# First norm and index tiles of a two-layer trunk, taken in halves of the features

## What is computed

```python
cond = silu(c)
mod = cond @ mod_w[i] + mod_b[i]
sh1, sc1, g1, sh2, sc2, g2 = jnp.split(mod, 6, axis=-1)
h = modulate(rms_norm(x, norm_mix_g[i]), sh1, sc1)   # norm * (1 + sc1) + sh1
proj = h @ w_in                                      # q, k, v, qi, ki, wi
logits = einsum(qi, ki) / 8                          # 8 index heads
score = sum over heads of wi * relu(logits)          # then the 64 best keys per query
```

## Time and profile before

| | |
|---|---|
| profiled execution | 809.15 us, span 807.1 us |
| PE / PEld busy | 744.8 us (92%) / 669.7 us (83%) |
| DVE / ACT / POOL busy | 595.7 (74%) / 389.5 (48%) / 208.2 us (26%) |
| DMA | 157.51 MB, mean 195 GB/s |
| chain that ended last | PE 64%, DVE 19%, issue 8%, ACT 6% |

### The profile page before, as it was taken

How to read it: one execution, slowest core, us unless ns; L and a number is a source line. 1 busy time by engine, 2 the same in 40 slices (tenths; PEclk the granted TensorE clock), 3 DMA queues, 4 the chain that set the end, 5 groups by cost and what they waited for, 6 DMA issues and landing times.

```text
span 807.1 us, 17682 instructions
## 1 busy us (share of the span) xinstructions
PE 744.8 (92%) x6676; PEld 669.7 (83%) x6676; DVE 595.7 (74%) x935; ACT 389.5 (48%) x651; POOL 208.2 (26%) x121
## 2 busy tenths in 40 slices
PE   4589999999899999999999888998999999999996
PEld 0176999667788989898989778997979999999994
DVE  7854555895778888888898886677557776676675
ACT  2254544555464444454444543334456555555554
POOL 5900000121315445544544234552000000000000
PEclk9789999999989999999999989999989999999998
DMA  8869655496726777777765311111644556555531
GB/s 313 345 224 369 215 182 182 184 411 262 266 79 249 251 258 258 260 260 256 256 247 175 134 53 54 54 54 62 201 131 131 184 182 198 168 180 192 171 102 53
DMA packets 45979, 157.51 MB, mean 195 GB/s; under 512 B 6257, under 2 KB 7793, under 8 KB 45937
## 3 DMA queue, kind: packets, MB, share of 16 engines
q1 hardware_dynamic: 43632, 148.55, 52.6%
q10 hardware_dynamic: 1728, 6.29, 2.0%
q0 software_dynamic: 576, 2.10, 0.7%
HBM read 155.87 MB, written 1.05 MB: 194 GB/s over the span
## 4 chain that ended last, share of the span: by engine, by line
PE 64%; DVE 19%; issue 8%; ACT 6%; DMA 2%; POOL 1%; DVEq 0%; ACTq 0%; POOLq 0%
PE up L326 11%; PE up L328 11%; PE up L327 11%; PE acc L326 7%; DVE wlo L978 7%; PE acc L327 7%; PE acc L328 7%; ACT whi L719 3%; PE gv L362 2%; DVE ffn L1232 2%; DMA ffn<-in_mw 1%; DVE hl L1007 1%; DVE diag L999 1%; PE up L667 1%; PE acc L642 1%
## 5 line engine op out<-in xcount | busy, mean ns | idle before, releaser
L978 DVE TENSOR_TENSOR wlo<-raw,whi 128x1024 fp32r<-128x1024 f32 x194 | 304.5, 1586 | 102.0 <-ACT whi L719 100.8
L326 PE MATMUL up<-hh,whi 128*128 128x256 f32 x944 | 272.0, 288 | 4.3 <-DVE hl L1007 3.0
L327 PE MATMUL up<-hl,whi 128*128 128x256 f32 x944 | 269.3, 285 | 0.0
L328 PE MATMUL up<-hh,wlo 128*128 128x256 f32 x944 | 269.2, 285 | 0.0
L719 ACT ACTIVATE whi<-raw 128x1024 fp32r<-128x1024 f32 x194 | 200.9, 1051 | 35.3 <-PE acc L328 24.4
L326 PEld LDWEIGHTS up<-hh,whi 128*128 128x128 f32 x944 | 183.5, 194 | 16.1 <-issue 11.1
L327 PEld LDWEIGHTS up<-hl,whi 128*128 128x128 f32 x944 | 183.7, 195 | 0.0
L328 PEld LDWEIGHTS up<-hh,wlo 128*128 128x128 f32 x944 | 183.4, 194 | 0.0
L326 PE MATMUL acc<-ah,whi 128*128 128x256 f32 x352 | 100.4, 285 | 6.8 <-DVE wlo L978 6.6
L327 PE MATMUL acc<-al,whi 128*128 128x256 f32 x352 | 99.6, 283 | 0.0
L328 PE MATMUL acc<-ah,wlo 128*128 128x256 f32 x352 | 99.5, 283 | 0.0
(11 more groups left out here) (200 smaller groups left out, 915.5 us busy)
## 6 DMA issues: line engine op xcount, KB each, us to landing
raw<-in_w SPq DMA_DIRECT2D x194, 512.0 KB, 3.5
mraw<-in_mw SPq DMA_DIRECT2D x60, 512.0 KB, 6.3
arena<-in_mw SPq DMA_DIRECT2D x12, 512.0 KB, 11.6
tmp<-in_mw SPq DMA_DIRECT2D x6, 512.0 KB, 7.9
ffn<-in_mw SPq DMA_DIRECT2D x6, 512.0 KB, 8.6
tmp<-in_mw ACTq DMA_DIRECT2D x4, 512.0 KB, 7.5
ffn<-in_mw ACTq DMA_DIRECT2D x4, 512.0 KB, 9.6
mraw<-in_mw ACTq DMA_DIRECT2D x4, 512.0 KB, 14.3
```

The source lines that it names most:

```text
L326: pe.matmul(out, w_h, xh, start=first, stop=False, skip_group_check=skip)
L327: pe.matmul(out, w_h, xl, start=False, stop=False, skip_group_check=skip)
L328: return pe.matmul(out, w_l, xh, start=False, stop=last, skip_group_check=skip)
L978: dve.tensor_tensor(wlo[:, n % SPL, :], raw[:, n % RAW, :], whi[:, n % SPL, :].bitcast(F32), ALU.subtract).then_inc(lo_ready, 1)
```

## The change

The first norm and the six index tiles are done for features 0 to 511 and then for 512 to 1,023. The chunks are reordered on the host, so that chunk 0 is the scale and chunk 1 the shift of the first half, and 2 and 3 those of the second. SP loads x first, then chunk 0, three small tensors, chunk 1, three more, the first halves of the six weight tiles, chunks 2 and 3, the second halves. The condition and the parameters are issued from ACT's queue. TensorE takes the norm ahead of gemv 0 and has a PSUM bank for each index tile (`idx_bank`), so that their first halves can stay there while gemv 2 and 3 run. GpSimd's six table steps now wait until all six index tiles are evicted, and ACT takes the sine in four pieces behind tiles 25 to 28. VectorE waits for the tables ahead of the attention masks, which lie on the same memory.

```diff
@@ -180,6 +180,9 @@
+        raw_half = raw[:].rearrange("p s (h c) -> p s h c", h=2)
+        whi_half = whi[:].rearrange("p s (h c) -> p (s h) c", h=2)
+        wlo_half = wlo[:].rearrange("p s (h c) -> p (s h) c", h=2)
@@ -206,6 +209,9 @@
+        first_hi, first_lo, first_used = sem("first_hi"), sem("first_lo"), sem("first_used")
+        ones_in = sem("ones_in")
+        w_first = [sem(f"w_first{j}") for j in range(RAW)]
@@ -242,8 +248,10 @@
-        N_PRM, N_EARLY, N_SMALL = 2, 6, 4
+        N_PRM, N_ONES, N_EARLY, N_SMALL = 2, 3, 3, 4
...
+        idx_bank = [acc[:, 0, 0:T], acc[:, 1, 0:T], acc[:, 2, 0:T], acc[:, 3, 0:T], up[:, 0, 0:T], up[:, 1, 0:T]]
@@ -263,19 +271,30 @@
-            sp_.dma_start(craw[:], t["cond"]).then_inc(cond_in, 16)
-            for dst, name in ((prm[:, 0:PRM_IN, :], "prm"), (jrow[:], "jrow")):
-                sp_.dma_start(dst, t[name]).then_inc(prm_in, 16)
-            load_m(0)
-            for dst, name in ((modb[:], "modb"), (ones[:], "ones"), (ident[:], "ident"), (gains[:], "gains"),
-                              (epsc[:], "epsc"), (picks[:], "picks")):
-                sp_.dma_start(dst, t[name]).then_inc(early_in, 16)
+            def load_half(n, h):
+                sp_.dma_start(raw_half[:, n, h, :], t["w"][n, :, 512 * h:512 * h + 512]).then_inc(
+                    (w_first, w_loaded)[h][n], 16)
+            def load_early(c):
+                for s in range((c - 1) * MS, c * MS):
+                    sp_.dma_start(early[:, s, :], t["mw"][MS + s, :, :]).then_inc(m_early[s], 16)
...
-            for s in range(3 * MS):
-                sp_.dma_start(early[:, s, :], t["mw"][MS + s, :, :]).then_inc(m_early[s], 16)
+            load_m(0)
+            for dst, name in ((ones[:], "ones"), (ident[:], "ident"), (epsc[:], "epsc")):
+                sp_.dma_start(dst, t[name]).then_inc(ones_in, 16)
+            load_early(1)
+            for dst, name in ((modb[:], "modb"), (gains[:], "gains"), (picks[:], "picks")):
+                sp_.dma_start(dst, t[name]).then_inc(early_in, 16)
...
-                load_w(n, free=False)
+                load_half(n, 0)
+            load_early(2)
+            load_early(3)
+            for n in range(RAW):
+                load_half(n, 1)
@@ -400,14 +419,16 @@
-                pe.wait_ge(gm_ready, pairs)
+                if pairs:
+                    pe.wait_ge(gm_ready, pairs)
...
-                pe.wait_ge(mod_col, pairs)
+                if pairs:
+                    pe.wait_ge(mod_col, pairs)
@@ -423,26 +444,36 @@
+            def half(n, h):
+                pe.wait_ge((first_lo, lo_ready)[h], n + 1)
+                for kk in range(4):
+                    k = 4 * h + kk
+                    pe.wait_ge(act_lo, k + 1)
+                    w_h, w_l = whi_half[:, n, kk * P:(kk + 1) * P], wlo_half[:, n, kk * P:(kk + 1) * P]
+                    pe.matmul(idx_bank[n], w_h, hh[:, k, :], start=(k == 0), stop=False, skip_group_check=True)
+                    pe.matmul(idx_bank[n], w_h, hl[:, k, :], start=False, stop=False, skip_group_check=True)
+                    mm = pe.matmul(idx_bank[n], w_l, hh[:, k, :], start=False, stop=(k == KT - 1), skip_group_check=True)
+                mm.then_inc((first_used, slot_used)[h], 1)
...
+            pe.wait_ge(ones_in, 16 * N_ONES)
+            pe.wait_ge(early_in, 16 * N_EARLY)
+            norm(0, 0, None)
...
+            spread_root(0, misc[:, T:2 * T])
...
-            pe.wait_ge(early_in, 16 * N_EARLY)
...
-            norm(0, 1, None)
+            for n in range(RAW):
+                half(n, 0)
+            pe.wait_ge(gm_ready, 1)
...
-            spread_root(0, up[:, 0, 0:T])
...
+            pe.wait_ge(hp_ready, 4)
...
-                if n >= 2:
-                    pe.wait_ge(qkv_ready, n - 1)
-                if n == 0:
-                    project_two((up[:, 0, 0:T], up[:, 1, 0:T]), 0, 0)
-                elif n > 1:
-                    project(up[:, n % 2, 0:T], n)
+                half(n, 1)
@@ -739,7 +770,8 @@
-                act.wait_ge(cols_done, 1 if norm == 0 else C_FFN // 2 if norm == 1 else CH)
+                if norm:
+                    act.wait_ge(cols_done, C_FFN // 2 if norm == 1 else CH)
@@ -754,31 +786,61 @@
+            act.dma_start(craw[:], t["cond"]).then_inc(cond_in, 16)
+            for dst, name in ((prm[:, 0:PRM_IN, :], "prm"), (jrow[:], "jrow")):
+                act.dma_start(dst, t[name]).then_inc(prm_in, 16)
...
+            for k in range(KT):
+                square(0, k)
...
+            act.wait_ge(ones_in, 16 * N_ONES)
+            root(0)
+            def first_half(n, h):
+                act.wait_ge((w_first, w_loaded)[h][n], 16)
+                if h:
+                    act.wait_ge(first_used, n + 1)
+                act.activation(whi_half[:, n, :], raw_half[:, n, h, :], ACT.Copy).then_inc((first_hi, hi_ready)[h], 1)
+            def first_in(k):
+                act.wait_ge(hp_ready, k + 1)
+                sh = 4 + k if k < 4 else 8 + k
+                act.activation(hh[:, k, :], tmp[:, k, :], ACT.Identity, bias=modc[:, sh:sh + 1]).then_inc(act_hi, 1)
+            act.wait_ge(csum, 1)
...
-            for k in range(KT):
-                square(0, k)
-            act.wait_ge(early_in, 16 * N_EARLY)
-            root(0)
+            first_half(0, 0)
+            first_half(1, 0)
+            act.wait_ge(mod_col, 1)
+            for k in range(4):
+                first_in(k)
+            for n in range(2, RAW):
+                first_half(n, 0)
...
-            for n in range(SPL):
-                split_hi(n, ring=False)
+            first_half(0, 1)
+            first_half(1, 1)
...
-            norm_hi(0, 0, 8)
+            for k in range(4, KT):
+                first_in(k)
+            for n in range(2, RAW):
+                first_half(n, 1)
...
-                act.activation(qkv[:, n, :], up[:, n % 2, 0:T], ACT.Copy).then_inc(qkv_ready, 1)
-                split_hi(n + SPL)
+                act.activation(qkv[:, n, :], idx_bank[n], ACT.Copy).then_inc(qkv_ready, 1)
+                if n % 2:
+                    act.wait_ge(w_loaded[n // 2], 16 * 2)
+                    act.activation(whi[:, n // 2, :], raw[:, n // 2, :], ACT.Copy).then_inc(hi_ready, 1)
@@ -793,13 +855,21 @@
-            act.wait_ge(tab_arg, TAB_STEPS)
-            act.activation(tab, tab, ACT.Sin, scale=TWO_PI * (1 - 2 ** -23)).then_inc(tab_ready, 1)
-            with act.Fori(1, N_IN // RAW) as i:
+            def tile_out(n, i=0):
+                act.wait_ge(slot_used, n + RAW * i + 1)
+                act.activation(qkv_f[:, ds((n + RAW * i) * T, T)], up[:, n % 2, 0:T], ACT.Copy).then_inc(qkv_ready, 1)
+                split_hi(n + SPL, i)
+            with act.Fori(1, N_IN // RAW - 1) as i:
...
-                    act.wait_ge(slot_used, n + RAW * i + 1)
-                    act.activation(qkv_f[:, ds((n + RAW * i) * T, T)], up[:, n % 2, 0:T], ACT.Copy).then_inc(qkv_ready, 1)
-                    split_hi(n + SPL, i)
+                    tile_out(n, i)
+            for n in range(N_IN - RAW, N_IN):
+                tile_out(n)
+                part = n - N_IN + RAW - 1
+                if 0 <= part < 4:
+                    act.wait_ge(tab_arg, TAB_STEPS)
+                    piece = tab[:, part * 1024:(part + 1) * 1024]
+                    act.activation(piece, piece, ACT.Sin, scale=TWO_PI * (1 - 2 ** -23)).then_inc(tab_ready, 1)
@@ -1009,7 +1079,7 @@
-                dve.wait_ge(amul_ready, norm + 1)
+                dve.wait_ge(amul_ready, norm + 2)
@@ -1077,25 +1147,47 @@
+            def first_half(n, h):
+                dve.wait_ge((first_hi, hi_ready)[h], n + 1)
+                dve.tensor_tensor(wlo_half[:, n, :], raw_half[:, n, h, :], whi_half[:, n, :].bitcast(F32),
+                                  ALU.subtract).then_inc((first_lo, lo_ready)[h], 1)
+            def first_scale(h):
+                dve.wait_ge(mod_col, h + 1)
+                dve.scalar_tensor_tensor(amul[:, 0, 4 * h:4 * h + 4], modc[:, 8 * h:8 * h + 4], 1.0,
+                                         gains[:, 0, 4 * h:4 * h + 4], ALU.add, ALU.mult).then_inc(amul_ready, 1)
+                dve.wait_ge(amul_ready, h + 1)
+                for k in range(4 * h, 4 * h + 4):
+                    scaled(0, k)
+            def first_low(k):
+                sh = 4 + k if k < 4 else 8 + k
+                dve.wait_ge(act_hi, k + 1)
+                dve.scalar_tensor_tensor(hl[:, k, :], tmp[:, k, :], modc[:, sh:sh + 1],
+                                         hh[:, k, :].bitcast(F32), ALU.add, ALU.subtract).then_inc(act_lo, 1)
...
-            col_out(0)
-            scale_columns(0, 0)
+            dve.wait_ge(ones_in, 16 * N_ONES)
...
-            dve.wait_ge(amul_ready, 1)
...
-            for k in range(KT):
-                scaled(0, k, up[:, 0, 0:T])
-            col_out(1)
-            split_lo(0)
-            split_lo(1)
-            for k in range(KT):
-                low_in(k, 0, 8)
```

(30 more changed lines are left out.)

## The result

The changed kernel takes 831.88 us (median of 4 runs, 830.26 to 833.12) against 811.02 for the kernel before (4 runs, 810.74 to 813.1); the ratio is 1.0257 (95% interval 1.0238 to 1.0275). The first norm and the first index tiles do begin earlier, and the whole gets 2.6% slower.

What follows compares the result with a forecast made beforehand. TensorE, fully busy from 86.5 to 144 us, carries any earlier delay to the end, and GpSimd and VectorE exclude each other. Front -1.6, index stage +21.5, clock +2.1: +22.0 on 809.15 gives 831; own range 822 to 837, reaching down to 818.

Steps and rivals of the forecast that it cites:

- The front's start: TensorE's square sums start once the three small early_in loads have landed behind x and chunks 0 and 1: 19.3 us.
- slow clock twice: Index tiles: the lower clock level at both sets of half tiles, each six costing 10.8 us; 2.3 us lost.
- sixth eviction: ACT's copy of the last of six index tiles out of PSUM, put at 66.8 us; before, 68.43.
- The gain of the front: Up to the sixth eviction: tiles start 12 us sooner but end only 1.6 us sooner.
- The stall: Index stage: VectorE alternates with GpSimd's table steps; split of tile 9 39.4 us after the sixth eviction, costing 21.5.
- The clock: Start of tile 9: TensorE's clock falls while it stands waiting, losing 2.1 us (bounds 0 and 2.4).
- Sum: Whole kernel: -1.6 front, +21.5 index stage, +2.1 clock, giving +22.0 us on the profiled 809.15.
- The sine: ACT's Sin leaves the index stage; its four pieces behind tiles 25 to 28 cost zero.
- Held to the end: Index stage: every table step keeps VectorE out for its whole length; four us more, 835; chance 0.12.
- GpSimd yields: Index stage: a VectorE chain that has the port keeps it to its end; 815 us; chance 0.08.
- Faster: Index stage: head accumulations not held, split of tile 9 within 19.5 us; 807 or 802.5 us; chance 0.06.
- the alternation of one VectorE operation per gap: Index stage: VectorE and GpSimd take turns, one VectorE operation between table steps; split of tile 9 at 39.4 us.

Runs made afterwards that it cites:

- half steps: The changed kernel with the six GpSimd table steps cut into 12 of 128x1024, in the same place: 811.80 us, ratio 1.0015.
- quarter steps: The changed kernel with the six GpSimd table steps cut into 24 of 128x512, in the same place: 811.22 us, ratio 0.9998.

## Why the prediction was right

The forecast was 831, the median is 831.88, and the steps it was made of can be held against the trace one by one.

- **The front's start** was put at 19.3 from the place of the loads in the queue; it was 19.36. The run with the small loads first shows that it was these loads.
- **First half tile** 34 (34.10), **second** 53.3 (54.28), the pause a new idle time of 4.9 (5.0 from 49.24 to 54.28, with columns in it), **slow clock twice** (0.50 both times), **sixth eviction** 66.8 (66.92). The gain of the front is 1.5 us, as forecast 1.6. That the eviction was met to 0.1 us is partly luck: the forecast had it held by ACT's issue of chunk 6, at 3.41 us until 66.5, and put less than two copies of 0.38 behind it. The issue took 1.94 and was over at 65.88, and the sixth copy waited for TensorE, which was through at 66.5 instead of 66.0. It had begun the second halves 1.0 us later than forecast, mostly because the first slow stretch held 27 matmuls (34.10 to 40.05) and not 23.
- **Whose gain it is.** The forecast booked the 1.6 for the front as a whole. With the tables moved alone the sixth eviction ends at 60.26: the tables' going is worth 8.2 us there, and the halves take 6.7 of it back.
- **The stall.** Split of tile 9 done 39.4 after the sixth eviction; measured 105.1 - 66.92 = 38.2, which is 20.3 us over the kernel before once TensorE's 0.8 in hand is off, where I had 21.5. The order was right down to the single operation: the split behind step 1, L1201 behind all of step 2, one L1204 behind step 3, four more by the start of step 5, two behind its opening. The first pass ended 27.4 after the eviction, not 28.8 (94.33 - 66.92). Of these 1.4 us, 0.4 had come by the end of step 3, and 0.5 came because step 4 ran at once instead of behind the first L1204. Another 0.5 came because steps 4 and 5 opened after 3.5 and 4.3 us, not 3.7 and 4.6: the forecast had read the opening from the ends of L1073 and L1061 without taking off their own 0.19. The second pass was as long as put, 7.9 us from the end of the relu (95.39 to 103.28).
- **The clock** after the stall: 15 matmuls in 3.4 us at 0.50 instead of some 28, 1.6 us; I had 2.1.
- **Sum**: -1.5 + 20.3 + 1.6 = 20.4. ACT's last eviction of the 30 tiles starts at 167.37 instead of 147.23, 20.1 later, and the medians differ by 20.9. The forecast of +22.0 was 1.1 too much, set on a profiled execution (809.15) that was 1.9 below the median of 811.02; the two errors nearly cancel, so that 831 came within 0.9 is in part luck.
- **Behind the 30 tiles.** The next 1.1 us appear in the attention, which the forecast had at its old length: from there to VectorE's first residual it is 53.5 us instead of 52.4 (199.68 before, 220.91 after). The other runs have 52.5 to 53.9 there, those with the sine in pieces at both ends of it, and the cause is open. The two profiled executions differ by 23.3: of this another 2.4 us lie between the same points of the state-space stage (451 to 554 us before, 473 to 578 after), where the granted clock was 0.93 and 0.90. The medians don't show it, and it comes and goes between profiled executions, whatever the kernel: from VectorE's first residual behind layer 0's feed-forward part to its first behind the state-space stage it is 110.1 us before (449.4 to 559.5) and 112.5 after (471.5 to 584.0), 110.1 with half steps, and 113.0 in the kernel before with later tables, which has no halves.
- **The sine** in pieces cost the input projection nothing, as put: from 108.5 to 166 TensorE is busy 57.50 of 57.50 us.

The rivals. *Held to the end* falls: single L1204 passed step 5 before its end, and others step 4. The Trainium skill, SBUF — State Buffer, "Who interferes with whom", says that whoever issues first has the pair for the whole instruction; the trace agrees, to 0.2 us, for steps with two tensors (4.79 us behind step 3) and not for a tensor_scalar step (4.3 of 7.09). *GpSimd yields* falls with the 15.41 us. *Faster* falls; its point, the split of tile 9 within 19.5 us, was 38.2.

Where my reasoning did not carry: the alternation of one VectorE operation per gap holds for steps of 2,048 columns. I took it to be a rule of the port and forecast 827 to 830 for quarter steps and 817 or more for half steps. They came out at 811.2 and 811.8. The cost is not the amount of table work but the width of a step, through two things: how long the longest closed stretch is, and how much of a step is the open tail.

What the halves themselves cost was seen in the forecast (5 of pause, 3.8 of gemv in the middle, 2.3 of clock against an earlier start), and the runs put a number on it: 11 us at the same place of the tables (812.06 against 801.14, and 822.44 against 811.40), of which 5.3 are the three small loads. Of the other 5.6, 4.0 are in the sixth eviction (63.0 against 59.0); the remaining 1.6 appears behind it, where the second pass begins 11.6 us after the eviction (74.62) instead of 10.0 (69.00). That this is chunk 5, asked for later relative to the eviction, is how I read it: its loads are issued 5.8 us before the eviction instead of 8.1 (57.21 to 63.0, 50.90 to 59.0), and ACT's copy of its row comes 8.7 us behind it instead of 7.0. It was not tried by itself. Nor was a version of the halves without the pause. (Between the profiled executions the small loads are worth 4.1 us at the sixth eviction, not 5.3; the medians of 10 and 5 runs leave room for either.)

## What to carry to other kernels

Before moving work to "free" GpSimd time, ask which VectorE operations then stand beside it: in these traces those with two operands in SBUF and tensor_scalar ones waited for its steps, and a chain of short ones waited again at nearly every step. If it must overlap, cut GpSimd's steps narrow first (here 128x1024 or less); that cost nothing and was worth 9 us in the old place (811.7 to 803.0) and 20 in the new one. And put the small tensors that gate the first matmul ahead of the megabytes that don't.

## What was not expected

- A GpSimd tensor_scalar of 2,048 or 1,024 columns lets VectorE in a fixed time before its end: 2.8 us for the two-operation form in whole and in half steps, 1.9 for the one-operation form (L1073 before ended at 27.56, less its own 0.19; the step at 29.24. In half steps an L1204 passed at 78.23, the step ended at 80.17). Quarter steps of 1.93 and 1.50 us are shorter than that and were open from 0.4 us on. Steps with two tensors were closed to 0.1 to 0.2 us before their end in every case looked at. The ends of GpSimd's entries are themselves rough, but they give the same lead each time.
- In half steps even VectorE's tensor_scalar passed at that point, which in whole steps had waited to the very end (1.25, 6.65 and 6.99 us). Why the width changes this is open.
- Not every VectorE operation waits. In the kernel before, the eight scaled tiles L1002, which read one operand from PSUM, started at 37.90 inside GpSimd's sixth step and took 3.22 us, 0.40 each, as they do in the changed kernel with nothing beside them (four in 1.66 at 31.30):

```profile
36.51 4.53 POOL L1413 TENSOR_TENSOR arena<-arena 128x2048 f32<-128x2048 f32 x1
```
